# Gating tables of four tokens, made and applied ahead of each of the last 64 up tiles of a two-layer expert kernel

## What is computed

```python
s1, s2 = q1 @ subkeys[0].T, q2 @ subkeys[1].T       # two 128-way scores, 8 heads
v1, i1 = top_k(s1, 16); v2, i2 = top_k(s2, 16)
cs, ci = top_k(v1[:, None] + v2[None, :], 16)       # the 16 best pairs of each head
e = i1[ci // 16] * 128 + i2[ci % 16]                # one of 128 * 128 experts
g = softmax(cs)
a = gelu(x @ u_tab[e].T)
y = (g * a) @ v_tab[e]
```

## Time and profile before

| | |
|---|---|
| median of 3 runs | 2908.99 us (2905.86 to 2910.26) |
| the profiled execution, its own time | 2908.07 us |
| its span, and mean granted clock of PE | 2905.8 us, 0.983 |
| PE busy | 2771.0 us (95%), 16662 matmul records |
| DVE / ACT / POOL busy | 1946.6 / 1486.4 / 1447.3 us |

### The profile page before, as it was taken

How to read it: one execution, slowest core, us unless ns; L and a number is a source line. 1 busy time by engine, 2 the same in 40 slices (tenths; PEclk the granted TensorE clock), 3 DMA queues, 4 the chain that set the end, 5 groups by cost and what they waited for, 6 DMA issues and landing times.

```text
span 2905.8 us, 53264 instructions
## 1 busy us (share of the span) xinstructions
PE 2771.0 (95%) x16662; PEld 2418.7 (83%) x16662; DVE 1946.6 (67%) x3521; ACT 1486.4 (51%) x2901; POOL 1447.3 (50%) x1137
## 2 busy tenths in 40 slices
PE   6999999997999999899999988999998999999998
PEld 6689999997777887789999986787878998876666
DVE  7736982338788887758940358888876544477776
ACT  1115554449645555455555568555545643255553
POOL 4831998888554441005989887544430000234442
PEclk8999999999999999899999999999999999999999
DMA  7634556770466663234555730766654533389994
GB/s 255 211 111 143 183 181 241 258 256 12 145 246 224 234 234 120 73 127 151 182 182 189 256 130 36 256 241 219 228 183 138 182 131 122 115 295 358 357 358 181
DMA packets 172454, 562.50 MB, mean 194 GB/s; under 512 B 15521, under 2 KB 18337, under 8 KB 172209
## 3 DMA queue, kind: packets, MB, share of 16 engines
q1 hardware_dynamic: 169968, 556.86, 54.6%
q10 hardware_dynamic: 2368, 4.19, 0.4%
HBM read 559.94 MB, written 1.05 MB: 193 GB/s over the span
## 4 chain that ended last, share of the span: by engine, by line
PE 59%; issue 19%; POOL 10%; ACT 7%; DVE 3%; DMA 1%; POOLq 0%; ACTq 0%; DVEq 0%; SPq 0%
PE bank L1094 20%; PE bank L1124 10%; PE bank L828 7%; PE bank L1417 6%; PE bank L887 5%; PE bank L1438 4%; ACT hT L1670 4%; POOL w_parts L2846 3%; ACT hT L1666 1%; POOL mean L2911 1%; POOL hT L2911 1%; DMA ring<-stream 1%; POOL mean L2913 1%; POOL hT L2913 1%; ACT h_parts L1678 1%
## 5 line engine op out<-in xcount | busy, mean ns | idle before, releaser
L2846 POOL TENSOR_TENSOR w_parts<-ring,w_parts 128x512 fp32r<-128x512 f32 x512 | 661.1, 1307 | 411.3 <-ACT w_parts L1630 378.2
L1094 PE MATMUL bank<-h_parts,w_parts 128*128 128x256 f32 x6144 | 751.8, 284 | 8.4 <-POOL w_parts L2846 6.1
L1094 PEld LDWEIGHTS bank<-h_parts,w_parts 128*128 128x128 f32 x6144 | 743.2, 192 | 9.4 <-issue 4.8
L1630 ACT ACTIVATE w_parts<-ring 128x512 fp32r<-128x512 f32 x512 | 320.0, 631 | 346.3 <-PE bank L1094 283.4
L1124 PE MATMUL bank<-h_parts,a_parts 128*128 128x512 f32 x1536 | 366.4, 394 | 8.1 <-DVE a_parts L2436 8.1
L1124 PE MATMUL bank<-w_parts,a_parts 128*128 128x512 f32 x1536 | 372.1, 398 | 1.3 <-DVE a_parts L2436 1.2
L1124 PEld LDWEIGHTS bank<-h_parts,a_parts 128*128 128x128 f32 x1536 | 284.6, 188 | 83.7 <-DVE a_parts L2436 25.3
L1124 PEld LDWEIGHTS bank<-w_parts,a_parts 128*128 128x128 f32 x1536 | 286.1, 190 | 62.4 <-DVE a_parts L2436 3.5
L1695 ACT ACTIVATE a_parts<-arena 128x256 fp32r (+1 forms) x256 | 107.0, 418 | 367.0 <-PE bank L1124 365.1
L828 PE MATMUL bank<-h_parts,w_parts 128*128 128x256 f32 x2304 | 282.5, 285 | 4.1 <-DVE w_parts L2027 4.1
L828 PEld LDWEIGHTS bank<-h_parts,w_parts 128*128 128x128 f32 x2304 | 279.7, 193 | 5.1 <-issue 4.4
(11 more groups left out here) (401 smaller groups left out, 4528.2 us busy)
## 6 DMA issues: line engine op xcount, KB each, us to landing
ring<-stream SPq DMA_DIRECT2D x594, 512.0 KB, 3.3
arena<-stream SPq DMA_DIRECT2D x105, 1024.0 KB, 7.3
arena<-stream SPq DMA_DIRECT2D x144, 512.0 KB, 4.5
hT<-stream SPq DMA_DIRECT2D x80, 512.0 KB, 4.4
mean<-stream SPq DMA_DIRECT2D x32, 512.0 KB, 4.5
arena<-consts ACTq DMA_DIRECT2D x1, 1536.0 KB, 6.5
xT<-xin ACTq DMA_DIRECT2D x1, 1024.0 KB, 10.7
out<-hT SPq DMA_DIRECT2D x4, 256.0 KB, 2.2
```

The costliest lines, as they stand in the source:

```text
L1094: mm = pe.matmul(bank[k][:, 0:T], w[:, wp, ws], h_parts[:, hp, 4 * j + q, :], start=(j == 0 and q == 0 and i == 0), stop=(j == 1 and q == ...
L1630: act.activation(w_parts[half % HALVES][:, 0, :], ring[slot_][:, j * 512:(j + 1) * 512], ACT.Copy).then_inc(sem(f"{n}_high"), 1)
L2846: pool.tensor_tensor(w[:, 1, :], ring[(base + k) % RING][:, j * 512:(j + 1) * 512], w[:, 0, :].bitcast(F32), ALU.subtract).then_inc(sem(f" ...
```

## The change

The table loop between up and down is gone. A table group of four tokens is made ahead of each of up tiles 64 to 127 (`TABLE_TILE` = 64): step s (0 to 63) handles tokens 4s to 4s + 3 and stands before tile 64 + s on PE. `W` of tiles 64 to 127 is first filled with ones (ACT fills 32 tiles during tiles 56 to 63, DVE the other 32), the table of a group is multiplied into all of `W`, and each tile's gelu is left by ACT in its bank and multiplied into `W` by DVE (`gate_tile`), after which later tables still multiply the tile's later tokens. DVE makes `hot1` with one instruction for each token and `hot2` of the even steps; for the odd steps POOL makes the difference and ACT takes `Abs` and `Relu` (`second_hot`). `hot1` now lies in `hT`, `hot2` in `a_parts`, with room for two groups each. The mod rows are done in eighths between the `hot1` instructions (`up_row_dve`), from half tiles of 256 KB.

```diff
+            def second_hot(count):
+                part = hot2[:, GROUP:2 * GROUP, :]
+                act.wait_ge(sem(f"{n}_diff2"), count)
+                act.activation(part, part.bitcast(F32), ACT.Abs).then_inc(sem(f"{n}_abs2"), 1)
+                act.wait_ge(sem(f"{n}_abs2"), count)
+                act.activation(part, part.bitcast(F32), ACT.Relu, scale=-1.0, bias=one_col).then_inc(sem(f"{n}_hot2"), 1)
...
+            second_hot(1)
+            with act.Fori(TABLE_TILE // 8, NK // 8 - 1) as it:
+                for k in range(8):
+                    gelu(None, k % 4, it * 16 + 2 * (k + 1), bank[k % 4][:, 0:T])
+                    high((k + 3) % 8, it * 16 + 2 * (k + 3), it * 32 + tile_at(k + 3), base)
+                    if k % 2:
+                        second_hot(it * 4 + (k // 2 + 2 - TABLE_TILE // 2))
...
+        def table_pe(pe, n, it, k, first):
+            pe.wait_ge(sem(f"{n}_hots"), it * 4 + (first + k + 1))
+            if k % 2:
+                pe.wait_ge(sem(f"{n}_hot2"), it * 2 + (first // 2 + k // 2 + 1))
+            pe.wait_ge(sem(f"{n}_applied"), it * 4 + (first + k + 1))
+            for s in range(GROUP):
+                slot_ = GROUP * (k % 2) + s
+                mm = pe.matmul(bank[4 + k % 2][:, s * P:(s + 1) * P], hot2[:, slot_, :].bitcast(F32), hot1[:, slot_, :],
+                               start=True, stop=True)
+            mm.then_inc(sem(f"{n}_tabled"), 1)
...
+            def make_hots(first, it, k, tokens):
+                at = it * 16 + GROUP * (first + k)
+                if tokens[0] == 0:
+                    dve.wait_ge(sem(f"{n}_tabled"), it * 4 + (first + k + 1))
+                for s in tokens:
+                    ins = dve.tensor_scalar(hot1[:, GROUP * (k % 2) + s, :], iota_p, route[:, 0, bass.ds(at + s, 1)],
+                                            route[:, 2, bass.ds(at + s, 1)], ALU.is_equal, ALU.mult)
...
+            def step(first, it, k, skip=False):
+                make_hots(first, it, k, (0, 1))
...
+                if not skip or k >= 1:
+                    apply_table(first, it, k - 1)
+                make_hots(first, it, k, (2, 3))
+                finish_hots(first, it, k)
+                if not skip or k >= 2:
+                    gate_tile(first, it, k - 2)
...
+            with pool.Fori(TABLE_TILE // 4, NK // 4) as it:
+                for k in range(4):
+                    if k % 2:
+                        pool.wait_ge(sem(f"{n}_tabled"), it * 4 + (k + 1 - TABLE_TILE))
+                        pool.tensor_tensor(hot2[:, GROUP:2 * GROUP, :], iota.unsqueeze(1).broadcast_to([P, GROUP, P]),
+                                           route[:, 1, bass.ds(it * 16 + GROUP * (k - TABLE_TILE), GROUP)].unsqueeze(2)
+                                           .broadcast_to([P, GROUP, P]), ALU.subtract).then_inc(sem(f"{n}_diff2"), 1)
+                    lows(it, k)
```

More of the change, by code:

```diff
@@ L1079, in peer_pe, with up_pe @@
             back_pe(pe, n, "kv" if l == 0 else "mid", {0: ((act_y, 1), (dve_y, 1)), 2: ((act_y, 2), (dve_y, 2))})
-        def up_pe(pe, l, first, last, rows=None):
+        def table_pe(pe, n, it, k, first):
[8 more added lines that the diff above has]
+            mm.then_inc(sem(f"{n}_tabled"), 1)
+        def up_pe(pe, l, first, last, rows=None, tables=None):
             n = f"p{l}"
@@ L1631, in high, with gelu @@
                                    ACT.Copy).then_inc(sem(f"{n}_high"), 1)
-            def gelu(i, k, count):
+            def gelu(i, k, count, out=None):
                 act.wait_ge(sem(f"{n}_half_free"), HALVES + count)
-                act.activation(W[:, i, :], bank[k][:, 0:T], ACT.Gelu).then_inc(sem(f"{n}_gelu"), 1)
+                act.activation(W[:, i, :] if out is None else out, bank[k][:, 0:T], ACT.Gelu).then_inc(sem(f"{n}_gelu"), 1)
             def tile_at(i):
@@ new lines, in peer_act @@
+            with act.Fori(0, ROUTE_TILE // 8) as it:
+                for k in range(8):
+                    gelu(bass.ds(it * 8 + k, 1), k % 4, it * 16 + 2 * (k + 1))
+                    high((k + 3) % 8, it * 16 + 2 * (k + 3), it * 32 + tile_at(k + 3), base)
+            act.wait_ge(sem(f"{n}_picked"), TT)
+            for i in range(ROUTE_TILE, TABLE_TILE):
+                gelu(slice(i, i + 1), i % 4, 2 * (i + 1))
+                if i == ROUTE_TILE:
+                    act.wait_ge(sem("turned"), TT * (l + 1))
+                at = TABLE_TILE + 4 * (i - ROUTE_TILE)
+                act.activation(W[:, at:at + 4, :].rearrange("p i (h n) -> p (i h) n", n=P), ones.unsqueeze(1).broadcast_to([P, 8, P]),
+                               ACT.Copy).then_inc(sem(f"{n}_ones"), 1)
+                high((i + 3) % 8, 2 * (i + 3), tile_at(i + 3), base)
@@ L1680, in down_high @@
+                if i % 2 and i + 2 < NK:
+                    second_hot((i + 2 - TABLE_TILE) // 2 + 1)
             def down_high(k, it=0):
@@ new lines, in up_row_dve @@
+            r = row % 2
+            total = bank[6][:, r * P:(r + 1) * P]
+            at = lambda n, per: it * (2 * per) + ((done + row) * per + n)
+            w = up_buffer(j // 4)[:, j % 4 * P:(j % 4 + 1) * P]
+            if j % 4 == 0:
+                dve.wait_ge(up_landed[j // 4], at(16, 16))
+            if j == 0:
+                dve.tensor_scalar(total, w, c[:, 0:1], None, ALU.mult).then_inc(sem("up_step"), 1)
+                return
+            if j == 4:
+                dve.wait_ge(sem("up_half"), at(1, 1))
+            else:
+                dve.wait_ge(sem("up_step"), at(j if j < 4 else j - 1, 6))
@@ new lines, in peer_dve @@
+            for k in range(4):
+                step(0, 0, k, True)
+            for first, turns in ((4, GROUPS // 8 - 1), (GROUPS // 2, GROUPS // 8)):
+                back = 1 if first == 4 else 0
+                with dve.Fori(back, turns + back) as it:
+                    for k in range(4):
+                        step(first - 4 * back, it, k)
+            apply_table(GROUPS, 0, -1)
+            gate_tile(GROUPS, 0, -2)
+            gate_tile(GROUPS, 0, -1, 1)
+            up_rows_dve(dve, l)
```

248 lines of the change are left out of this document (92 added, 156 removed).

## The result

The changed kernel takes **2988.3 us** (median of 4 runs, 2985.8 to 2991.5), the kernel before 2907.4 us on the same chip (4 runs, 2905.3 to 2910.3): a ratio of **1.028**, 95% interval 1.026 to 1.030. Slower by 81 us, where 82 were forecast. Its profiled execution has a span of 2989.7 us, 83.9 more than the one before, at a mean granted clock of 0.976.

A forecast was written before the change was run, and what follows sets the result against it. PE was taken as the bound. Tables and tiles, mod columns, odd-step waits and down's start gave 331.7 against 293.1 us (layer 0) and 328.7 against 284.9 (layer 1): +82.4 on 2908.07, forecast 2991 us, range 2945 to 3085.

The forecast's parts named there:

- The wait at odd steps: PE stands before odd tables while ACT does a half, `Abs`, `Relu`: 2.15 us, 31 a layer, 66.7 us a layer.
- The faster rival: Odd steps' `hot2` is ready when PE comes, so no wait at odd tables: total 2857 us; chance 12%.
- half way case: `half_free` count off by one half, ACT starts 1.44 us sooner: 0.7 us of wait left, about 2901 us.
- Table and tile on PE: Each step on PE is a table group of 1.12 us plus a tile of 2.88: 4.00 us, 256.0 for 64 steps.
- The lower bound of 0.96 for a group: A group of eight table records on PE at the up tiles' spacing of 0.120 us: 0.96 us.
- the prediction's own sign: Prediction called itself wrong if, among other things, the group of 8 records on PE isn't near 1.1 us.
- The clock: PE's granted clock in the new stage expected to stay at 1.00, the 2.4 GHz level.
- a fall of the whole stage as a rival: PE at 1.2 GHz in the new stage: 4.00 us longer a step, 512 us in all; chance 2%.
- the inference from the table loop before: Old loop has PE busy 62 of 80 us at clock 1.00, so the new stage was expected at that level.
- DVE: DVE's work for two steps with mod rows: 6.6 us against 10.15 on PE, so it doesn't bound.
- The rival of 0.60 us for each: Small DVE instructions with fresh addresses cost 0.60 us, making DVE the bound: +91, total 3082 us; chance 7%.
- The ends: Stage's start and end: fills hidden at no cost; last up tile to first down matmul 4.5 and 3.8 us.

The follow-up runs named there:

- Version 1: Changed kernel with `second_hot` (ACT's `Abs` and `Relu`) moved ahead of both halves of `high`: 2826.4 us, 0.9729 of the kernel before.
- version 5: Changed kernel with `second_hot` placed between the two halves of `high` on ACT: 2884.2 us, 0.9932 of the kernel before.
- version 8: Changed kernel with `second_hot` ahead of both halves and two of four table matmuls left out: 2781.5 us, 0.9583 of the kernel before.

## Why the prediction was right, point by point

The stretch from tile 64 to the first down matmul is 332.9 us in layer 0 (464.13, where the first table could start, to 797.00; 331.7 was forecast) and 1889.12 - 1559.63 = 329.5 in layer 1 (328.7). Together they grew by 39.8 + 44.6 = 84.4 us, for 82.4 forecast. Beneath so close a sum the terms moved:

- **The wait at odd steps**, the term that decides: right in place, number (31 a layer) and size, 2.15 us of 2.15, 66.7 us a layer. Version 1 shows the cause: change the order and it is gone. The faster rival needed a `Relu` that PE doesn't wait for; the time that it gives, 2857, was too high for it by 27 us, as version 1 shows (0.9729 of the 2909 us that the forecast starts from is 2830). Its half way case, a stall of 0.7 us and some 2901 us, was too high as well: version 5 has 0.72 us and 0.9932 of before, 2889.
- **Table and tile on PE**: 8.14 us for two steps with a column were forecast, 7.86 measured. The group was sized at 1.12 us from a spacing of 0.14; it holds PE for 0.81 to 0.91. The tile was sized at 2.88 and is 2.96. Together that is 9.0 and 10.2 us too much a layer. The lower bound of 0.96 for a group was not low enough, and by the prediction's own sign (a group near 1.1 us, a pair of 10.1 to 10.3) this term was wrong. The Trainium skill's 81 ns for 128 columns ("TensorE: Matmul & The Clock Gate", "Back-to-back issue gap") makes 0.65, which is too low here: the trace lies between that page and the spacing of the loop before, at 0.10 to 0.11 us.
- **The clock**: forecast at 1.00, with only a fall of the whole stage as a rival. It fell in 5 and 6 of the pairs, 7.7 and 9.3 us. The step that failed was the inference from the table loop before, where gaps of 1.05 us in every 5.7 left the clock at 1.00: that the share of idle time is alike says nothing about gaps twice as long. The Trainium skill ("TensorE: Matmul & The Clock Gate", "A second HAM failure mode: psum-queue depth-cycling") tells of short idling between groups that makes the clock swing. The stage's trace agrees with it in that short idling made the clock swing, at 0.6% of the kernel's time, though the idling here is a wait for ACT; the table loop's didn't.
- **DVE**: forecast at 6.6 us for two steps, not the bound; measured some 7.1 (version 8), not the bound. A `hot1` is followed after 0.32 to 0.33 us, not 0.26. In the even step 2.4 of 2.7 us were forecast in use; from the start of the table's application (545.90) to the end of `hot2` (548.35) it takes 2.45, and PE comes 0.25 us later, so that two more instructions made it wait 0.39. The rival of 0.60 us for each is out.
- **The ends**: down's start was forecast at 4.5 and 3.8 us and took 5.6 and 5.5, because POOL, whose first mod row load has landed by then, works beside DVE's first instructions. DVE's first table in layer 0 came 1.25 us late: the fill was hidden, as forecast, but the sum had DVE start its `hot1` during tiles 56 to 63, and the increment for that stands behind them on PE. The wait of 1.16 us for POOL in tiles 56 to 63, which the prediction left as it was, is gone: tile 64 could start at 464.13, for 465.62 before.

In layer 0 the forecast of 331.7, less 9 for tables and tiles, plus 7.7 for the clock, 1.25 for the first table and 1.1 for down's start, is 332.8. In layer 1 (whose first half has no columns, so that even groups take 0.81) it is 328.7 - 10.2 + 9.3 + 1.7 = 329.5. So the term that decides was right by its mechanism, but that the total came out within 3 us was luck in part: errors of 10 us with opposite signs met.

## What to carry to other kernels

Before work is put on a queue, ask what stands ahead of it and what releases that: an instruction that the bounding engine needs at once must not stand behind one that waits for what this engine has only just finished. The same two ACT instructions, ahead of the two halves instead of behind them, turn a kernel 2.8% slower than before into one 2.7% faster. And a wait on PE is not worth its length alone: price it at its length only where a trace shows the clock at 1.00 with waits as long as that one.
